# Rows of four experts gathered in one product, and an expert loop of period four on TensorE

## The chip, the cores and the metric

The kernel runs on one core of one Trainium2 chip. The metric is the device time of one execution in microseconds (us). A core has a matrix engine (TensorE; in the profile PE for its products and PEld for its weight loads), VectorE (DVE), ScalarE (ACT), GpSimd (POOL), and SyncE (SP), which here only issues transfers. Sixteen DMA engines move data between HBM and the on-chip memory (SBUF). TensorE writes to eight banks of a second memory (PSUM), 128 partitions by 512 floats each. The engines run their own instruction streams and wait for each other by semaphores.

## The reference

Two layers of a backbone block: three token mixers (which the change leaves alone), then a mixture of experts. The model width is 1024. Layer 0 works on 512 tokens (256 latent, 256 context), layer 1 on 256. Each token goes to two of 32 experts; an expert is a gated product of width 512. Cut to the expert part:

```python
weights = p_grp * top_p                       # two weights for each token
experts = g_top * EXP_PER_GROUP + top_i       # two of 32 experts
xs = h_pad[token_of_slot].reshape(n_blk, MOE_BLK, D)     # rows in the order of the experts
def run_block(args):
    xb, e = args
    return (silu(xb @ w_gate[e]) * (xb @ w_up[e])) @ w_down[e]
ys = lax.map(run_block, (xs, block_expert)).reshape(n_slots, D)
out = zeros((T, D)).at[order // TOP_K].add(ys[dest] * w_sorted[:, None])
```

An expert's weights are 1024 x 1024 (gate and up side by side) and 512 x 1024 floats, 6.3 MB; 32 experts in two layers make 403 MB.

## The kernel before

After the mixers and the router, the normalized token rows stand in SBUF twice, as a rounded part `hr_hi` and a rest `hr_lo` (128 tokens to a tile, `nt` = 4 tiles in layer 0 and 2 in layer 1). `place1` holds for each token and expert the token's place among that expert's rows. Experts are worked on in order, and the first 64 rows (`BLK`) of each are the normal case. Weights stand in two slots: expert e uses slot e % 2, in pieces of 1 MB (four of `wgu` and two of `wd`).

Around each pair of experts:

- VectorE makes `pick` (L1571), a one-hot matrix for each token tile of 2 x 64 columns: column j is the token at place j of the expert.
- TensorE `pick_x` (L761): `pick` stands in the array and row halves of 512 columns move, so that 128 rows (64 of each expert) come to banks 0 and 7, slots on partitions. VectorE copies them to `xs` (L1582, L1583).
- TensorE `turn_x` (L770) turns them into model width on partitions, eight turns of 128 x 128, and VectorE copies the two banks to `xg` (L1586, L1587).

For each expert TensorE does `gate_up` (L777: 64 instructions, 32 weight loads and 32 products), half of the next pair's pick or turn, `turn_h` (L789, 4 instructions) of the hidden rows that ScalarE (L1202) and VectorE (L1645) made, the other half, and `down` (L794, 32 instructions). For the next pair the even expert (s = 0) picks (32 instructions in layer 0) and the odd one (s = 1) turns (16). The two are the body of TensorE's loop (L889), 16 times a layer. ScalarE copies the result (L1206) and sends it to `y_rows` in HBM (L1154).

If an expert has more than 64 rows (L859), `more_slots` (L807) works on 32 further rows at a time before `gate_up`, with waits between its steps: 242 array instructions in layer 0. The body is written out once for rows 65 to 96, and again in a loop for those beyond, which is skipped if there are none (L868). In the profiled execution this path ran four times (L1185, count 4): for experts 17 and 20 of layer 0 and 2 and 7 of layer 1, once each.

SyncE's loop (L460) asks for the weights two experts ahead. Before each piece it waits until TensorE has used that piece of the slot (`gu_used`, L452, and `down_used`, L457). The weights of experts 0 and 1 are asked for at the end of the mixers (L446).

Ahead of a loop stand, on TensorE, `pick_x` and `turn_x` for the first pair (L848 to L852) and, on VectorE, the remaining routing steps (L1597 to L1610). Behind it GpSimd fetches the rows of `y_rows` (L1767).

Of the kernel before, what the change touches and what calls it, by code (L numbers as in the profile page):

```python
# [27 lines left out]
P = 128  # L28
# [27 lines left out]
AHEAD = 4  # L56
PAIRS = NE // 2
LATENT, CONTEXT = slice(0, SEQ), slice(SEQ, NTOK)
# [78 lines left out]
def hybrid_block(nc, t, out, counts=None):  # L137
# [4 lines left out]
    with ctx:  # L142
# [49 lines left out]
        def part(base, kib, size, *dims, dt=F32):  # L192
# [21 lines left out]
        xg, xs = part(ht_flat, 8, 4, KC, P), part(ht_flat, 12, 4)  # L214
# [3 lines left out]
        pick = placed("pick", [P, 4, 2 * BLK], ARENA_AT + 38 * 1024, F32R)  # L218
        ysb, ysb_o = part(arena, 40, 2), part(arena, 42, 1)
# [48 lines left out]
            hr_hi_set hr_lo_set r_exp r_onehot r_pos r_exp_done routed pick_set picko_set dest_set xs_done xs_copied xt_done xt_copied  # L268
# [203 lines left out]
        def _(pe):  # L472
# [115 lines left out]
            for l in range(DEPTH):  # L588
# [172 lines left out]
                def pick_x(half):  # L761

                    for tile in range(nt):
                        for rows in (hr_hi, hr_lo):
                            mm = pe.matmul(ps[:, 7 * half, :], pick[:, tile, :], rows[:, tile, 512 * half:512 * half + 512],  # L765
                                           start=(tile == 0 and rows is hr_hi), stop=(tile == nt - 1 and rows is hr_lo))
                    if half:
                        mm.then_inc(g["xs_done"].sem, 1)

                def turn_x(half):  # L770
                    for c in range(4):
                        at = (4 * half + c) * P
                        mm = pe.transpose(ps[:, 7 * half, c * P:(c + 1) * P], xs[:, at:at + P], ident[:, :])
                    if half:
                        mm.then_inc(g["xt_done"].sem, 1)

                def gate_up(s, slot, landed):  # L777
# [29 lines left out]
                def more_slots(more, slot, landed, s, two):  # L807
# [27 lines left out]
                    for k in range(4):  # L835
                        if k % 2 == 0:
                            pe.wait_ge(wd_in[s][k // 2].sem, (PAIRS * l + two + 1) * 16)
                        for j in range(4):
                            mm = pe.matmul(ps[quarters[j], 6, 0:256], hid_t_o[:, quarters[k]], wd[s][k // 2][:, k % 2, 256 * j:256 * j + 256],
# [6 lines left out]
                pair0, pick0 = (PAIRS + 1) * l, (PAIRS + 2) * l  # L846
# [7 lines left out]
                def expert(e, two, s):  # L854
                    done, landed, slot = NE * l + e, PAIRS * l + two + 1, s
                    n = pe.value_load(n_of[0:1, bass.ds(e, 1)], min_val=0, max_val=NTOK)
                    pe.wait_ge(g["xt_copied"].sem, pair0 + two + 1)
                    pe.nop(nofuse=True)
                    with pe.If(n > BLK):  # L859
                        if s:  # L860
                            pe.wait_ge(g["xs_copied"].sem, pair0 + two + 2)

                        def more_block(b):
                            more_slots(pe.snap(n_more, min_val=0, max_val=64), slot, landed, s, two)
                            pe.reg_add(n_more, n_more, 1)

                        more_block(BLK // MORE)
                        with pe.If(n > BLK + MORE):  # L868
                            with pe.Fori(BLK // MORE + 1, w_all // MORE) as b:
                                with pe.If(n > b * MORE):  # L870
                                    more_block(b)
                                pe.nop(nofuse=True)
# [991 lines left out]
```

## Time and profile before

| | us |
|---|---|
| median of 3 runs | 2012.0 |
| the three | 2002.98, 2012.0, 2014.25 |
| span of the profiled execution | 2003.0 |

| engine | busy us | share |
|---|---|---|
| TensorE products | 1775.8 | 89% |
| TensorE weight loads | 1006.8 | 50% |
| VectorE | 693.7 | 35% |
| ScalarE | 521.1 | 26% |
| GpSimd | 155.9 | 8% |

The page cuts the span into 40 slices of 50 us. The tenths of the DMA engines' busy share and the rate show where transfers fill the time:

```profile
DMA  8346555322345999999999443334388999999993
GB/s 317 132 169 230 190 206 207 110 73 90 100 165 223 421 421 421 421 420 415 408 421 420 146 132 98 100 106 146 121 354 310 421 421 420 421 421 421 420 420 135
```

Slices 13 to 21 are layer 0's expert loop, 30 to 38 that of layer 1. Of the costliest groups these belong to it (line, engine, operation, output<-input, count | busy us, mean ns | idle time before and its cause):

```profile
L784 PE MATMUL ps<-moe,ht 128*64 128x512 f32 x2048 | 473.2, 604 | 57.9 <-DMA moe<-in_w_exp_gate_up_dram 43.5
...
L800 PE MATMUL ps<-moe,arena 128*64 128x512 f32 x1024 | 233.8, 598 | 2.5
...
L765 PE MATMUL ps<-hr_hi,pick 128*128 128x512 f32 x204 | 88.9, 436 | 9.7 <-DVE pick L1571 9.7
L765 PE MATMUL ps<-hr_lo,pick 128*128 128x512 f32 x204 | 82.4, 404 | 0.0
```

Products overlap each other, so the distance between two starts says more than the duration of one. "issue" is time in which an engine waited for nothing that the profile shows.

### The profile page before, as it was taken

The numbers are of one execution on the slowest core, as the hardware profiler recorded it, in microseconds if no ns is written. First come the engines' busy times: TensorE is split into PE (matmuls) and PEld (weight loads), VectorE is DVE, ScalarE is ACT, GpSimd is POOL, SyncE is SP. The second block draws the span as 40 slices with busy tenths as digits, with TensorE's granted clock in tenths as the row PEclk, the third lists the DMA queues.
The fourth block names the chain that finished last, engine by engine and source line by source line (L and its number), as shares of the span: only waits on it lengthen the run. The fifth ranks groups of instructions, "written<-read, shape, count | busy, mean of one in ns | idle before, by whom it ended". The sixth has DMA issues, their size and how long they took to land.

```text
span 2003.0 us, 26586 instructions
## 1 busy us (share of the span) xinstructions
PE 1775.8 (89%) x9291; PEld 1006.8 (50%) x9292; DVE 693.7 (35%) x1455; ACT 521.1 (26%) x1061; POOL 155.9 (8%) x190
## 2 busy tenths in 40 slices
PE   6999899989986999989999599999969999888884
PEld 3766566668753443334343487778823333222322
DVE  3465355444533111111111665673441111111113
ACT  4344444442321111001111454452311111011011
POOL 0063031000000000000000224320000000000000
PEclk9999999999988999999999799999979999999997
DMA  8346555322345999999999443334388999999993
GB/s 317 132 169 230 190 206 207 110 73 90 100 165 223 421 421 421 421 420 415 408 421 420 146 132 98 100 106 146 121 354 310 421 421 420 421 421 421 420 420 135
DMA packets 96048, 550.55 MB, mean 275 GB/s; under 512 B 14162, under 2 KB 15650, under 8 KB 42724
## 3 DMA queue, kind: packets, MB, share of 16 engines
q1 hardware_dynamic: 83108, 526.89, 66.6%
q0 software_dynamic: 4224, 11.35, 2.0%
q10 hardware_dynamic: 8640, 11.28, 1.6%
q8 instruction: 50, 0.82, 0.2%
q14 instruction: 26, 0.21, 0.0%
HBM read 537.15 MB, written 12.32 MB: 274 GB/s over the span
## 4 chain that ended last, share of the span: by engine, by line
PE 65%; DMA 14%; DVE 8%; SPq 5%; ACT 4%; issue 3%; POOL 0%; ACTq 0%; POOLq 0%; DVEq 0%
PE ps L784 14%; DMA moe<-in_w_exp_gate_up_dram 12%; PE ps L493 8%; PE ps L800 8%; PE ps L495 8%; PE ps L494 8%; PE ps L765 4%; SPq L412 3%; PE ps L715 2%; PE ps L642 2%; PE ps L671 2%; PE ps L653 2%; SPq L417 1%; DMA moe<-in_w_mod_dram 1%; DVE w_lo L1302 1%
## 5 line engine op out<-in xcount | busy, mean ns | idle before, releaser
L784 PE MATMUL ps<-moe,ht 128*64 128x512 f32 x2048 | 473.2, 604 | 57.9 <-DMA moe<-in_w_exp_gate_up_dram 43.5
L784 PEld LDWEIGHTS ps<-moe,ht 128*64 128x64 f32 x2048 | 140.9, 138 | 379.6 <-issue 258.7
L1645 DVE TENSOR_TENSOR arena<-aux,ps 128x256 f32<-128x256 f32 x64 | 26.9, 421 | 673.2 <-ACT aux L1202 673.2
L493 PE MATMUL ps<-ht_hi,w_hi 128*128 128x512 f32 (+1 forms) x704 | 252.3, 358 | 2.0 <-ACT arena L1089 1.6
L495 PE MATMUL ps<-ht_hi,w_lo 128*128 128x512 f32 (+1 forms) x704 | 243.7, 346 | 0.0
L494 PE MATMUL ps<-ht_lo,w_hi 128*128 128x512 f32 (+1 forms) x704 | 243.5, 346 | 0.0
L800 PE MATMUL ps<-moe,arena 128*64 128x512 f32 x1024 | 233.8, 598 | 2.5
L1302 DVE TENSOR_TENSOR w_lo<-ws,w_hi 128x1024 fp32r<-128x1024 f32 (+1 forms) x122 | 149.5, 1230 | 222.4 <-ACT w_hi L994 222.3
L994 ACT ACTIVATE w_hi<-ws 128x1024 fp32r<-128x1024 f32 (+1 forms) x122 | 125.2, 1026 | 180.1 <-PE ps L495 146.1
L493 PEld LDWEIGHTS ps<-ht_hi,w_hi 128*128 128x128 f32 x704 | 133.2, 189 | 24.4 <-issue 8.6
L495 PEld LDWEIGHTS ps<-ht_hi,w_lo 128*128 128x128 f32 x704 | 133.1, 189 | 16.9
L494 PEld LDWEIGHTS ps<-ht_lo,w_hi 128*128 128x128 f32 x704 | 133.4, 189 | 15.3
L1206 ACT ACTIVATE arena<-ps 128x512 f32<-128x512 f32 x64 | 38.2, 597 | 370.5 <-PE ps L800 370.5
L800 PEld LDWEIGHTS ps<-moe,arena 128*64 128x64 f32 x1024 | 67.8, 136 | 131.3 <-issue 111.4
L1767 POOL DMA_INDIRECT arena<-y_rows,dest x8 | 8.0, 1001 | 1447.1 <-ACTq L1221 1445.3
L1202 ACT ACTIVATE aux<-ps 128x256 f32<-128x256 f32 x64 | 24.6, 385 | 335.4 <-PE ps L784 335.4
L765 PE MATMUL ps<-hr_hi,pick 128*128 128x512 f32 x204 | 88.9, 436 | 9.7 <-DVE pick L1571 9.7
L765 PE MATMUL ps<-hr_lo,pick 128*128 128x512 f32 x204 | 82.4, 404 | 0.0
L1202 ACT ACT_TABLE_LOAD x32 | 41.1, 1283 | 134.4 <-issue 134.4
L765 PEld LDWEIGHTS ps<-hr_hi,pick 128*128 128x128 f32 x204 | 39.6, 194 | 42.3 <-issue 30.7
L1750 POOL DMA_DIRECT2D aux<-in_rpb_a_dram x64 | 39.8, 634 | 181.2 <-DVE stat L1420 127.5
L653 PEld LDWEIGHTS ps<-ident,moe 128*128 128x128 f32 x320 | 35.0, 143 | 34.4 <-issue 32.6
(252 smaller groups left out, 2159.1 us busy)
## 6 DMA issues: line engine op xcount, KB each, us to landing
moe<-in_w_exp_gate_up_dram SPq DMA_DIRECT2D x256, 1024.0 KB, 20.7
moe<-in_w_exp_down_dram SPq DMA_DIRECT2D x128, 1024.0 KB, 21.4
ws<-in_w_in_dram SPq DMA_DIRECT2D x92, 512.0 KB, 4.2
moe<-in_w_mod_dram SPq DMA_DIRECT2D x29, 1536.0 KB, 6.5
y_rows<-arena ACTq DMA_DIRECT2D x164, 64.0 KB, 5.6
ws<-in_w_branch_dram SPq DMA_DIRECT2D x16, 512.0 KB, 3.5
ws<-in_w_out_dram SPq DMA_DIRECT2D x16, 512.0 KB, 3.6
arena<-in_w_mod_dram SPq DMA_DIRECT2D x3, 1536.0 KB, 19.3
```

Of the source, the lines that this page charges most:

```text
L412: sp.dma_start(wgu[slot][i], e_src(t["w_exp_gate_up"])[:, 2 * i:2 * i + 2]).then_inc(gu_in[slot][i].sem, 16)
L493: pe.matmul(ps[:, bank, 0:cols], w[:, k, :], a_hi, start=(i == 0), stop=False)
L494: pe.matmul(ps[:, bank, 0:cols], w[:, k, :], a_lo, start=False, stop=False)
L495: mm = pe.matmul(ps[:, bank, 0:cols], w_lo[:, slot, k, :], a_hi, start=False, stop=(k == rows[-1]))
L642: mm = pe.matmul(score_bank[:, hh, 0:n], q_of(kind)[HD * hh:HD * hh + HD, pair, q0:q0 + P], kt_of(kind, 2 * pair + hh)[:, keys], start=Tru ...
L653: mm = pe.transpose(prob_bank[:, tile, hh * P:(hh + 1) * P], prob[h % 2][:, hh, tile * P:(tile + 1) * P], ident[:, :])
L765: mm = pe.matmul(ps[:, 7 * half, :], pick[:, tile, :], rows[:, tile, 512 * half:512 * half + 512], start=(tile == 0 and rows is hr_hi), st ...
L784: mm = pe.matmul(ps[BLK * j:BLK * j + BLK, 2, :].rearrange("p (g n) -> p g n", g=2), xg[:, k, BLK * s:BLK * s + BLK], w[k // 2][:, k % 2, ...
L800: mm = pe.matmul(ps[BLK * j:BLK * j + BLK, bank, :], src[:, k % 2, BLK * (k // 2):BLK * (k // 2) + BLK], w[k // 2][:, k % 2, 512 * j:512 * ...
L994: nc.scalar.activation(high_part(i)[:, 0:m], ws[:, slot, 0:m, :], ACT.Copy) \
L1202: nc.scalar.activation(act_g, ps[:, 2, 0:256], ACT.Silu).then_inc(g["silu_done"].sem, 1)
L1302: v.tensor_tensor(w_lo[:, ws_slots[item], 0:m], ws[:, ws_slots[item], 0:m, :], high_part(i)[:, 0:m].bitcast(F32), ALU.subtract).then_inc(g ...
```

## The change

`pick` becomes 4 x 64 columns (`set_four`), and a product now has 128 columns of the rows standing in the array and the 256 one-hot columns moving. The output is already turned: model width on partitions, the slots of four experts in the columns. `turn_x`, `xs` and the copies to it are gone. The eight chunks of the model width are gathered two for each expert (`gather(2 * s)`, `gather(2 * s + 1)`). VectorE holds six of them in `xg_next` and at the fourth expert copies them to `xg` and the last two from PSUM. `gate_up` of the first of four waits for `xg` piece by piece. TensorE's and VectorE's loops have period four; ScalarE's and SyncE's stay at two. On TensorE the large-expert path is now written once, in one loop over all steps of 32 rows from 64 on (14 steps in layer 0, 6 in layer 1), each with its own test. On VectorE and ScalarE it stays as it was.

```diff
-AHEAD = 4
+FOUR = 4
+AHEAD = 2 * FOUR
...
-                def pick_x(half):
+                def gather(chunk):
+
+                    bank, at = 7 * (chunk // 2 % 2), FOUR * BLK * (chunk % 2)
                     for tile in range(nt):
                         for rows in (hr_hi, hr_lo):
-                            mm = pe.matmul(ps[:, 7 * half, :], pick[:, tile, :], rows[:, tile, 512 * half:512 * half + 512],
+                            mm = pe.matmul(ps[:, bank, at:at + FOUR * BLK], rows[:, tile, chunk * P:(chunk + 1) * P], pick[:, tile, :],
...
+                            if s == 0:
+                                pe.wait_ge(g["xg_set"].sem, turned + k // 2 + 1)
...
-                pick_x(0)
-                pick_x(1)
-                pe.wait_ge(g["xs_copied"].sem, pair0 + 1)
-                turn_x(0)
-                turn_x(1)
...
+                for chunk in range(KC):
+                    if chunk in (4, 6):
+                        pe.wait_ge(g["xg_set"].sem, gathered + chunk // 2 - 1)
+                    gather(chunk)
...
-                    pe.wait_ge(g["xt_copied"].sem, pair0 + two + 1)
                     pe.nop(nofuse=True)
                     with pe.If(n > BLK):
                         if s:
...
+                            pe.wait_ge(g["xg_held"].sem, QUADS * FOUR * l + 4 * four + s)
+                        else:
+                            pe.wait_ge(g["xg_set"].sem, gathered + 4 * four + 4)
+                        pe.nop(nofuse=True)
+                        with pe.Fori(BLK // MORE, w_all // MORE) as b:
+                            with pe.If(n > b * MORE):
+                                more_slots(pe.snap(n_more, min_val=0, max_val=64), slot, landed)
+                                pe.reg_add(n_more, n_more, 1)
+                            pe.nop(nofuse=True)
                         pe.nop(nofuse=True)
                     pe.nop()
-                    gate_up(s, slot, landed)
+                    gate_up(s, slot, landed, gathered + 4 * four)
                     if s == 0:
-                        pe.wait_ge(g["pick_set"].sem, pick0 + two + 2)
+                        pe.wait_ge(g["pick_set"].sem, pick0 + four + 2)
                     else:
-                        pe.wait_ge(g["xs_copied"].sem, pair0 + two + 2)
-                    next_pair = turn_x if s else pick_x
-                    next_pair(0)
+                        pe.wait_ge(g["xg_held"].sem, QUADS * FOUR * l + 4 * four + s)
+                    gather(2 * s)
                     pe.wait_ge(g["hid_done"].sem, done + 1)
                     turn_h(hid)
-                    next_pair(1)
+                    gather(2 * s + 1)
...
-                with pe.Fori(0, PAIRS) as two:
-                    for s in range(2):
-                        expert(2 * two + s, two, s)
+                with pe.Fori(0, QUADS) as four:
+                    for s in range(FOUR):
+                        expert(FOUR * four + s, four, s)
...
-                set_pair(0)
-                dve.wait_ge(g["xs_done"].sem, pair0 + 1)
-                copy_xs()
-                set_pair(2)
-                dve.wait_ge(g["xt_done"].sem, pair0 + 1)
-                copy_xg()
+                def gathered_rows(p):
+                    return ps[:, 7 * (p % 2), :].rearrange("p (k n) -> p k n", n=FOUR * BLK)
+
+                done0 = 4 * (QUADS + 1) * l
+                set_four(0)
+                for p in range(4):
+                    dve.wait_ge(g["xg_done"].sem, done0 + p + 1)
+                    v.tensor_copy(xg[:, 2 * p:2 * p + 2, :], gathered_rows(p)).then_inc(g["xg_set"].sem, 1)
+                set_four(FOUR)
...
-                    if s == 0:
-                        dve.wait_ge(g["xs_done"].sem, pair0 + two + 2)
-                        copy_xs()
-                    else:
-                        dve.wait_ge(g["xt_done"].sem, pair0 + two + 2)
-                        copy_xg()
-                        set_pair(e + 3)
...
+                    if s < 3:
+                        dve.wait_ge(g["xg_done"].sem, done0 + 4 * four + s + 5)
+                        v.tensor_copy(xg_next[:, 2 * s:2 * s + 2, :], gathered_rows(s)).then_inc(g["xg_held"].sem, 1)
+                        return
+                    dve.wait_ge(g["xg_held"].sem, QUADS * FOUR * l + 4 * four + 3)
+                    for p in range(3):
+                        v.tensor_copy(xg[:, 2 * p:2 * p + 2, :], xg_next[:, 2 * p:2 * p + 2, :]).then_inc(g["xg_set"].sem, 1)
+                    dve.wait_ge(g["xg_done"].sem, done0 + 4 * four + 8)
+                    v.tensor_copy(xg[:, 6:8, :], gathered_rows(3)).then_inc(g["xg_set"].sem, 1)
+                    dve.sem_inc(g["xg_held"].sem, 1)
+                    set_four(e + FOUR + 1)
```

## Rows read from the trace of the kernel before

**Rows 1.** Stages: length; busy PE, PEld, DVE, ACT, POOL (x count); clock; DMA share; GB/s

```profile
614.00:617.00 3.00, 3.00 (x8) 2.32 (x8) 0.00 (x0) 0.00 (x0) 0.00 (x0) 0.50 0.00 0
...
641.00:650.00 9.00, 7.77 (x38) 2.48 (x36) 0.61 (x2) 0.60 (x1) 0.00 (x0) 1.00 0.87 310
...
653.00:767.00 114.00, 112.08 (x526) 45.90 (x528) 21.83 (x41) 13.59 (x21) 0.00 (x0) 1.00 1.01 421
...
941.00:961.00 20.00, 20.00 (x92) 8.19 (x92) 2.13 (x4) 2.65 (x4) 0.00 (x0) 1.00 1.00 373
...
1521.00:1533.00 12.00, 10.89 (x113) 4.61 (x107) 0.58 (x2) 2.23 (x4) 0.00 (x0) 0.94 0.32 103
...
1560.00:1958.00 398.00, 355.14 (x1675) 124.03 (x1675) 64.35 (x127) 43.87 (x69) 0.00 (x0) 1.00 1.01 421
```

**Rows 2.** The chain that ended last, in order of time: start, length, what

```profile
613.12 6.12 PE ps L765 x16
...
672.31 6.89 PE ps L784 x32
...
684.72 6.87 PE ps L784 x32
...
886.41 7.04 PE ps L784 x32
...
1070.62 26.32 DMA moe<-in_w_exp_gate_up_dram
...
1528.06 7.02 PE ps L784 x32
```

**Rows 3.** SyncE's queue, DMA issues: start, length of the issues, what

```profile
630.58 6.11 SPq L412 DMA_DIRECT2D moe<-in_w_exp_gate_up_dram  x4
...
942.93 5.48 SPq L412 DMA_DIRECT2D moe<-in_w_exp_gate_up_dram  x4
...
1530.12 5.46 SPq L412 DMA_DIRECT2D moe<-in_w_exp_gate_up_dram  x4
```

**Rows 4.** Queue 1 in 612-888, 612-943, 1480-1605 us: packets, MB, share of engines

```profile
q1 hardware_dynamic: 14159, 103.16, 90.4%
q1 hardware_dynamic: 17209, 125.39, 91.5%
q1 hardware_dynamic: 5810, 42.34, 84.8%
```

**Rows 5.** TensorE's products in order of time

```profile
680.12 0.44 PE L791 MATMUL ps<-ident,arena 128*128 128x128 f32 x2 [0.35 <-DVE arena L1645]
...
1445.60 0.28 PE L493 MATMUL ps<-mt_hi,w_hi 128*128 128x256 f32 x1
...
1445.72 0.28 PE L494 MATMUL ps<-mt_lo,w_hi 128*128 128x256 f32 x1
```

**Rows 6.** The one-hot tile's line: ns min/median/max of its two forms, 256 and 512 columns

```profile
L1571 DVE TENSOR_TENSOR pick<-arena,slots x36: 414/553/692, 612.4 to 1962.9; 128x512 fp32r<-128x512 f32 x18, 128x256 fp32r<-128x256 f32 x18
```

**Rows 7.** TensorE's sequencer, branch over the large path: before experts 0, 0, 1; ns, start

```profile
L859 PEldq COMPARE_BRANCH  x1: 3389/3389/3389, 623.2 to 623.2; - x1
L859 PEldq COMPARE_BRANCH  x1: 2796/2796/2796, 1478.3 to 1478.3; - x1
L859 PEldq COMPARE_BRANCH  x1: 6275/6275/6275, 1493.2 to 1493.2; - x1
```

**Rows 8.** TensorE's sequencer, back edge at 654 us, and the inner branch: ns, start

```profile
L889 PEldq ALU_OP  x1: 32/32/32, 654.1 to 654.1; - x1
L889 PEldq COMPARE_BRANCH  x1: 228/228/228, 654.2 to 654.2; - x1
L889 PEldq FUSED_REGOPS  x1: 63/63/63, 654.6 to 654.6; - x1
L868 PEldq COMPARE_BRANCH  x4: 208/210/213, 885.0 to 1601.6; - x4
```

**Rows 9.** Instruction queue from 612 to 660 us: packets, MB, share of engines

```profile
q8 instruction: 5, 0.08, 0.7%
```

More of the change, by code:

```diff
@@ L217, in hybrid_block @@
         pick_o = placed("pick_o", [P, 4, MORE], ARENA_AT + 37 * 1024, F32R)
-        pick = placed("pick", [P, 4, 2 * BLK], ARENA_AT + 38 * 1024, F32R)
-        ysb, ysb_o = part(arena, 40, 2), part(arena, 42, 1)
+        pick = placed("pick", [P, 4, FOUR * BLK], ARENA_AT + 38 * 1024, F32R)
+        ysb, ysb_o = part(arena, 42, 2), part(arena, 45, 1)
         xs_o, xg_o = aux[0:MORE, 2:4, :].rearrange("p a b -> p (a b)"), part(arena, 44, 1)
@@ L759, in _, with gate_up @@
                 pe.wait_ge(g["hr_lo_set"].sem, g["hr_lo_set"].at(l, 2 * nt - 1))
-                def pick_x(half):
+                def gather(chunk):
+                    bank, at = 7 * (chunk // 2 % 2), FOUR * BLK * (chunk % 2)
                     for tile in range(nt):
                         for rows in (hr_hi, hr_lo):
-                            mm = pe.matmul(ps[:, 7 * half, :], pick[:, tile, :], rows[:, tile, 512 * half:512 * half + 512],
+                            mm = pe.matmul(ps[:, bank, at:at + FOUR * BLK], rows[:, tile, chunk * P:(chunk + 1) * P], pick[:, tile, :],
                                            start=(tile == 0 and rows is hr_hi), stop=(tile == nt - 1 and rows is hr_lo))
[L767 to L777, printed above, removed]
+                    if chunk % 2:
+                        mm.then_inc(g["xg_done"].sem, 1)
+                def gate_up(s, slot, landed, turned):
                     w = wgu[slot]
@@ L805, in _, with more_slots @@
                 quarters = [slice(MORE * j, MORE * j + MORE) for j in range(4)]
-                def more_slots(more, slot, landed, s, two):
+                def more_slots(more, slot, landed):
                     pe.wait_ge(g["picko_set"].sem, more + 1)
@@ L883, in expert @@
                     turn_h(hid)
[L884 removed]
+                    gather(2 * s + 1)
                     pe.wait_ge(g["hidt_copied"].sem, done + 1)
                     pe.wait_ge(g["y_copied"].sem, done + 1)
[L887 to L891 removed]
+                    down(4, hid_t, slot, landed)
+                with pe.Fori(0, QUADS) as four:
+                    for s in range(FOUR):
+                        expert(FOUR * four + s, four, s)
@@ L1616, in _, with expert @@
                     dve.reg_mov(n_more, 0)
-                def expert(e, two, s):
+                def expert(e, four, s):
                     done = NE * l + e
@@ L1647, in expert @@
                     v.tensor_copy(hid_t, ps[:, 1, 0:256].rearrange("p (c n) -> p c n", n=P)).then_inc(g["hidt_copied"].sem, 1)
-                    if s == 0:
-                        dve.wait_ge(g["xs_done"].sem, pair0 + two + 2)
-                        copy_xs()
-                    else:
-                        dve.wait_ge(g["xt_done"].sem, pair0 + two + 2)
-                        copy_xg()
-                        set_pair(e + 3)
-                with dve.Fori(0, PAIRS) as two:
-                    for s in range(2):
-                        expert(2 * two + s, two, s)
+                    if s < 3:
[9 more added lines that the diff above has]
+                    set_four(e + FOUR + 1)
+                with dve.Fori(0, QUADS) as four:
+                    for s in range(FOUR):
+                        expert(FOUR * four + s, four, s)
                 def add_tile(tile):
```

42 lines of the change are left out of this document (13 added, 29 removed).

## The prediction

> **What bounds the kernel now.** I read the 40 slices of the page first, then the busy time by stage, then the chain that ended last, then the instructions of each queue. The change touches only the two expert loops (about 613 to 1105 us and 1470 to 1966 us). In them the DMA engines are full: their share is 1.01 at 421 GB/s from 653 us to the end of layer 0's loop and from 1560 to 1958 us [rows 1]. An expert brings six pieces of 1.05 MB, so at 421 GB/s (its output rows travel in the same stream) it takes 14.9 us. TensorE needs 12.4 us for an odd expert (672.31 to 684.72) and some 2 us more for an even one, and the chain near a loop's end is a transfer of gate/up weights that TensorE waits for (at 1070.62) [rows 2]. So inside the loop a TensorE microsecond is worth nothing in itself. It counts only where the transfers run dry, since a piece is asked for only when TensorE has used its slot. The rows to see are three places. At the start of a loop nothing moves until the first slot is released (630.58, [rows 3]). Around the third expert of layer 1, which has more than 64 rows, the DMA share is 0.32 for 12 us [rows 1], and the next release is at 1530.12 [rows 3]. Around expert 20 of layer 0 (941 to 961 us) the rate dips to 373 GB/s [rows 1].
>
> How much was still in flight at such a place: before the release at 888.47, 17 experts had been asked for since 612 us, 107.0 MB, of which 103.2 had moved by 888 [rows 4]: 3.8 MB or 9 us in hand. At 942.93 it was 20 experts, 125.8 MB against 125.4: 1 us in hand, and the 20 us that follow lose 20*(421-373)/421 = 2.3 us. At the second large expert of layer 1 (number 7), 44.0 MB against 42.3: 4 us in hand.
>
> **The change, part by part.** All against the profiled execution (span 2003.0 us, itself the fastest of the three times; the median is 9 us above it, so a shift in the trace is applied to 2012).
>
> *Gather in place of pick and turn.* For four experts of layer 0, TensorE now issues 2*16 products of 512 columns and 2*8 turns; after it, 64 products of 256 columns. A 256-column product of this type follows its predecessor by 0.12 us at full clock [rows 5], so a chunk of eight costs 0.96 us (0.48 in layer 1), two chunks an expert. The first chunk runs while ScalarE and VectorE make the hidden rows, a time in which today's four turns leave the array idle for 0.35 us (at 680.12, [rows 5]). From the odd expert's 12.4 us an expert then comes to about 12.7 us in layer 0 and 12.5 in layer 1. That saves 3 us for every four experts, which the full DMA hides: 0. VectorE's three extra copies and its one-hot tile of 1024 columns end within the 3.6 us of the down product, except before an odd large expert; 0.4 us there.
>
> *Start of a loop, layer 0.* The first one-hot tile grows from 512 to 1024 columns. By the two forms of its line (0.41 and 0.69 us, [rows 6]) that is 1.2 us, so +0.5. [...] After, 64 products start at 613.6: 18 at the low clock (0.24 us) and 46 at 0.12, together 9.9, to 623.5, and the copies run beside them. Now the jump over the code of the large-expert path follows. Its branch started at 623.2, behind the wait for the copies, and took 3.39 us [rows 7], which is why the experts began at 626.6. In steady state the sequencer is 1 to 3 us ahead of the array (the loop-count branch at 885.0 runs 1.4 us before the product at 886.41, [rows 2, 8]), and the new order has no wait ahead of the jump. I take 3 us of it as hidden: first product at 624.1, at the high clock, first release 2.0 us later instead of 3.9: 626.1 against 630.58, -4.4. Nothing hidden and a low clock would give +1. From 641 to 650 us the transfers lost 2.4 us (310 GB/s, [rows 1]) because the second expert also waited for code; I give back 1.6. Layer 0's start: -6.
>
> *The empty iterations.* The body for rows beyond 64 was written twice and the loop around the second was skipped. Now there is one body in a loop of 14 steps (6 in layer 1), of which only one works: 13 (or 5) empty steps on TensorE's queue for each large expert. No row shows one. A step is one taken branch over the body (208 ns), a nop, a register operation (32 ns) and the branch back (208) [rows 8]: 0.5 us by durations. By starts, the loop's own back edge (operation at 654.1, next instruction at 654.6, [rows 8]) takes 0.5 alone, which makes a step 0.9. I take 0.7, the middle. The last products cover 1.4 us. So a large expert costs TensorE 13*0.7-1.4 = 7.7 us more in layer 0 and 5*0.7-1.4 = 2.1 in layer 1. With 0.5 it is 5.1 and 1.1, with 0.9 it is 10.3 and 3.1. Nothing below zero: instructions are only added.
>
> [...]
>
> Layer 0: expert 17 has 9 us in hand and loses 7.7: about nothing. Expert 20 comes later by 7.7, less 1.4 for three quicker experts, plus 0.4 and its own 7.7: its release moves from 942.93 to 957.3. Transfers restart some 1.7 us later at 959.0. Before, they went on as if from 944.0+2.3 = 946.3: +12.7. Layer 0 in all: -6+12.7+0.2 (the last expert's second chunk is 0.3 us longer) = +6.9.
>
> *Layer 1.* The gather is 32 products: 18 at 0.24 and 14 at 0.12, 6.0 us from 1470.0 to 1476.0. The branch took 2.80 us from 1478.3 [rows 7]. In the new order its predecessors are held by the copy of the second pair, to about 1475.7, so it ends at 1478.5, against 1481.1. Expert 0 then runs at the high clock: 12.5. The jump to expert 1 took 6.28 us [rows 7] over two bodies; over one I take 4, of which 3 lie under the down product: +1.1, against 3.6. Experts 0 and 1 end at 1504.6 instead of 1515.1. The large path takes 12.5 + 0.3 + 2.1: expert 2's product at 1519.5 instead of 1528.06 [rows 2]: -8.6. As the transfers had run dry there, all of it counts. With the jumps fully exposed and the low clock it would be +0.5, with both hidden -12. Expert 7 has 4 us in hand and is later by 2.1 + 1.4 (first jump to the fourth copy of the code) - 1: it loses about 1.5. Layer 1: -7.
>
> Sum: +6.9-7.1 = -0.2; nothing else moves. Forecast 2011 us, the profile near 2002.
>
> **The rivals.**
> First, *empty steps are hidden* and cost under 0.4 us. Then no large expert matters: layer 0 gives -6 and the 2.3 us dip back, -8; layer 1 -9: 17 us faster, 1995. For it: the sequencer is seen ahead of the array. Against it: the branch rows.
>
> Second, slower: *a step costs 1.1 us*, as branch and nop each refill the queue. A large expert is 12.9 us in layer 0. Its release at expert 20 moves by 2*12.9-1.0 = 24.8 and the restart by 23.1; expert 17's 9 us are gone too. Layer 0 +17, layer 1 (4.1 per large expert) -3: 14 us slower, 2026. It decides from about 1.0 us a step, just above the 0.9 of the rows.
>
> Third, *the start gains nothing*: the code jumps stay exposed behind the gather. Layer 0 then is +13 and layer 1 near -3, if the warm clock stays: +9, 2021.
>
> Fourth, *the longer loop no longer stays in TensorE's instruction memory*. Now five 16 KB instruction packets come in 612 to 660 us [rows 9] and none from 660 to 1060 us, so the two-expert loop stays. It has some 1,220 array instructions; four experts with one body each have about 1,500. If each expert's jump cost 3.6 us again, it would take 16.3 instead of 14.9 us, 1.4*64 = 90 us slower, 2100. [...]
>
> **How the numbers follow.** Forecast (2011, own range 2002 to 2020): 0.52. Hidden steps 0.16, dear steps 0.17, no gain at the start 0.10, code not resident 0.05. A measurement of this kernel can tell about 0.5%, 10 us, from no change. Faster: the first rival and 0.03 of the forecast's edge, 0.19. Slower: the second and fourth and a little of the third and of the edge, 0.26. Same: 0.55. The range reaches from 1995 to the second rival: 1994 to 2027. It leaves out the fourth rival and the ends of the others.
>
> **What would show it.** In the profile after: 256-column products 0.12 us apart; the first release in layer 0 near 626 and in layer 1 an expert-2 product near 1519; a DMA share of 1.01 for the rest; a hole of some 8 to 12 us before expert 20's release in layer 0 and gaps of several us between the last product of the large path and the gate/up product behind it, 13 branch records each; no instruction packets in the middle of a loop. The forecast is wrong if those gaps are under 3 or over 11 us, if the first expert still starts 3 us behind the last gather, or if instruction packets recur.

## The result and the profile after

| | before | after |
|---|---|---|
| median of 9 runs each, us | 2011.4 (2003.0 to 2014.3) | 2016.7 (2015.4 to 2020.4) |
| span of the profiled execution | 2003.0 | 2014.6 |

The ratio is 1.0035, interval 1.0024 to 1.0046: the change costs 0.35%, 5 to 9 us. I had forecast 2011 and no change. The time lies within the range and within 0.5% of before, but it is measurably slower, and two large terms lie behind the small sum. Layer 0's loop lost twice what I had allowed; layer 1's gained what I had said. The experiments below remove the loss, and the kernel is then 0.8 to 1% faster than before.

The page of the kernel after (tenths and rate in 40 slices of 50.4 us; the instruction queue; the gate/up products):

```profile
DMA  8346555323246999997999533334488999999993
GB/s 315 131 168 229 194 201 213 105 68 100 89 186 255 419 420 421 421 398 318 372 420 421 224 111 100 95 110 131 136 352 318 421 410 421 421 421 421 420 421 137
...
q8 instruction: 52, 0.85, 0.2%
...
L782 PE MATMUL ps<-moe,ht 128*64 128x512 f32 x2048 | 476.8, 603 | 85.2 <-DMA moe<-in_w_exp_gate_up_dram 59.1
```

Three slices in layer 0 leave the full rate: 398, 318 and 372 GB/s stand from 857 to 1008 us, with the large experts 17 and 20 in them. Nothing else of note has moved. The chain of waits in order of time (start, length, what) tells why:

```profile
614.55 9.79 PE ps L768 x64
...
883.17 9.07 issue
892.24 8.56 PE ps L782 x32
...
932.27 3.84 PE ps L811 x16
...
945.60 1.93 PE ps L837 x32
947.53 8.87 issue
956.40 8.90 PE ps L782 x32
...
1488.11 6.04 PE ps L768 x32
...
1507.17 2.41 issue
1509.58 8.81 PE ps L782 x32
...
1535.62 2.79 issue
1538.41 7.11 PE ps L782 x32
```

Behind each large path (L837 is its last line) TensorE stands still for 9 us in layer 0 and 2.8 in layer 1. (The 2.41 us at 1507.17 are something else: the jump to expert 1, whose branch is shown at the end.) Before, the product behind it followed at once: 886.41 there [rows 2] answers to 892.24 here, and 940.88 to 956.40. From the same chain before, the product behind expert 20's large path, which started at 925.95:

```profile
940.88 7.02 PE ps L784 x32
```

TensorE's sequencer in the first gap (operation, count, ns min/median/max, first and last start):

```profile
L862 PEldq COMPARE_BRANCH  x14: 86/218/222, 882.4 to 892.1; - x14
...
L862 PEldq FUSED_REGOPS  x13: 35/35/35, 882.6 to 891.6; - x13
...
L863 PEldq COMPARE_BRANCH  x13: 214/214/214, 882.7 to 891.7; - x13
```

Thirteen branches over the body (L863) and the loop's own tests (L862): the empty steps. From the first to the last are 12 steps in 9.0 us, 0.75 us each. Thirteen make 9.75, and 9.07 of it shows, so the products in flight cover 0.7 us. Then SyncE's queue, the first issue after the releases of the first expert and of 17 and 20 of layer 0, the first and the last of which answer to [rows 3]:

```profile
626.37 5.47 SPq L414 DMA_DIRECT2D moe<-in_w_exp_gate_up_dram  x4
...
895.85 5.46 SPq L414 DMA_DIRECT2D moe<-in_w_exp_gate_up_dram  x4
...
960.26 5.55 SPq L414 DMA_DIRECT2D moe<-in_w_exp_gate_up_dram  x4
```

And the stretches around the gaps (length; busy PE, PEld, DVE, ACT, POOL; granted clock; DMA share; GB/s):

```profile
883.00:892.00 9.00, 0.17 (x4) 0.00 (x0) 0.00 (x0) 0.38 (x1) 0.00 (x0) 0.80 1.01 420
892.00:896.00 4.00, 3.76 (x12) 1.26 (x14) 0.00 (x0) 0.00 (x0) 0.00 (x0) 0.59 0.69 287
...
956.00:960.00 4.00, 3.60 (x10) 1.17 (x12) 0.00 (x0) 0.00 (x0) 0.00 (x0) 0.50 0.00 0
```

Two things are to be seen. Expert 17's gap is bridged by transfers in flight (share 1.01 up to 892), with nothing left over: the rate falls as the gap ends, and around expert 20, where nothing is in hand, the transfers stand (share 0.00) until the release at 960.26. And the products behind the gap run at a granted clock of 0.59 and 0.50, after TensorE had stood idle: microsecond by microsecond it is 1.00 up to 888 us, 0.50 from 889 to 895 and 1.00 again from 896; in the second gap it is 1.00 up to 949 and 0.50 from 950 to 960. That is why the gate/up products took 8.56 and 8.90 us where they took 7.04 and 7.02 before, and it was in none of my terms.

### The profile page after: what moved, and what is told of

Read it like the earlier page. It is cut to its first block, busy times and chain, and to the rows that moved or that the text cites. A ratio compares the mean times of both kernels' runs of the same rounds, so it can differ in the third digit from the quotient of the medians.

```text
span 2014.6 us, 26958 instructions
## 1 busy us (share of the span) xinstructions
PE 1764.4 (88%) x9475; PEld 1017.7 (51%) x9476; DVE 671.9 (33%) x1423; ACT 521.1 (26%) x1061; POOL 155.1 (8%) x190
## 4 chain that ended last, share of the span: by engine, by line
PE 60%; DMA 17%; SPq 7%; DVE 7%; issue 4%; ACT 4%; POOL 0%; ACTq 0%; POOLq 0%; DVEq 0%
DMA moe<-in_w_exp_gate_up_dram 15%; PE ps L782 11%; PE ps L495 8%; PE ps L497 8%; PE ps L496 8%; PE ps L798 7%; SPq L414 4%; PE ps L768 3%; SPq L419 2%; PE ps L717 2%; PE ps L644 2%; PE ps L673 2%; PE ps L655 2%; DMA moe<-in_w_mod_dram 1%; PE ps L553 1%
## 5 line engine op out<-in xcount | busy, mean ns | idle before, releaser
L798 PE MATMUL ps<-moe,arena 128*64 128x512 f32 x1024 | 235.5, 602 | 1.3
L496 PEld LDWEIGHTS ps<-ht_lo,w_hi 128*128 128x128 f32 x704 | 134.5, 191 | 15.3
L768 PE MATMUL ps<-pick,hr_hi 128*128 128x256 f32 x432 | 124.2, 316 | 10.5 <-DVE pick L1564 10.5
L798 PEld LDWEIGHTS ps<-moe,arena 128*64 128x64 f32 x1024 | 68.2, 137 | 123.1 <-issue 105.8
L768 PEld LDWEIGHTS ps<-pick,hr_hi 128*128 128x128 f32 x432 | 84.4, 195 | 62.6 <-issue 57.0
L768 PE MATMUL ps<-pick,hr_lo 128*128 128x256 f32 x432 | 111.5, 287 | 0.0
L768 PEld LDWEIGHTS ps<-pick,hr_lo 128*128 128x128 f32 x432 | 84.8, 196 | 0.0
```

What stands on the lines that cost most here:

```text
L496: pe.matmul(ps[:, bank, 0:cols], w[:, k, :], a_lo, start=False, stop=False)
L768: mm = pe.matmul(ps[:, bank, at:at + FOUR * BLK], rows[:, tile, chunk * P:(chunk + 1) * P], pick[:, tile, :], start=(tile == 0 and rows is ...
L798: mm = pe.matmul(ps[BLK * j:BLK * j + BLK, bank, :], src[:, k % 2, BLK * (k // 2):BLK * (k // 2) + BLK], w[k // 2][:, k % 2, 512 * j:512 * ...
```

## How the spans divide

I cut each profile at the start of the first one-hot product of a layer and at the start of the layer's last down product. For the kernel before these are 613.12, 1100.82, 1469.75 and 1961.71 us.

| kernel | span | layer 0's loop | between | layer 1's loop |
|---|---|---|---|---|
| before | 2003.0 | 487.7 | 368.9 | 492.0 |
| before again (e8) | 2006.0 | 488.5 | 370.8 | 492.3 |
| after | 2014.6 | 503.0 | 370.6 | 485.0 |
| e1 after, loop bounded by n | 1991.2 | 482.5 | 370.2 | 480.5 |
| e11 the same again | 1992.0 | 482.5 | 370.7 | 480.4 |
| e5 before, loop bounded by n | 1991.2 | 483.3 | 369.2 | 484.7 |
| e12 the same again | 1998.8 | 484.4 | 375.2 | 483.8 |
| e2 before with empty steps | 2017.0 | 504.4 | 369.3 | 488.7 |
| e4 after, twice the empty steps | 2048.8 | 522.1 | 374.4 | 498.7 |
| e9 after, short products in the gap | 2020.9 | 503.3 | 373.0 | 489.4 |
| e10 e1 and 0.95 us more an expert | 1995.2 | 485.4 | 370.3 | 483.2 |

## The experiments

My theory after the result: the gather does what it should, and the empty steps of the rewritten large-expert loop cost more than it gives. The rivals: the gather itself (64 and 32 small products, more copies) is dear; the longer code is; or TensorE's extra time in the full-rate stretches counts after all.

### The empty steps taken away (e1, e11)

```diff
-                        with pe.Fori(BLK // MORE, w_all // MORE) as b:
-                            with pe.If(n > b * MORE):
-                                more_slots(pe.snap(n_more, min_val=0, max_val=64), slot, landed)
-                                pe.reg_add(n_more, n_more, 1)
+                        with pe.Fori(BLK, n, MORE):
+                            more_slots(pe.snap(n_more, min_val=0, max_val=64), slot, landed)
+                            pe.reg_add(n_more, n_more, 1)
```

The loop now ends at the expert's own number of rows, read from the register, and needs no test inside. The rest of the change stays.

> The changed kernel, but the loop of the large path ends at the expert's own row count (start 64, end n, step 32) and has no test inside: no empty steps, one body. Theory (the empty steps, 13 or 5 of 0.75 us each, and the low clock behind them are what the change lost): the gap of some 9 us behind the large path is gone in layer 0 and that of 2.7 us in layer 1; layer 0's last transfer lands about 5 us earlier than in the kernel before, layer 1 gains about 11 us; span near 1987 against 2003.0 before and 2014.6 after, ratio to before about 0.992. Rival (the gather of narrow products or the loop of period four costs the time): the span stays above 2003.

Measured: 1991.4 us, ratio 0.990 (0.9883 to 0.9918). The chain of e1 has no gap behind the large paths of layer 0:

```profile
881.72 2.02 PE ps L837 x32
883.74 7.02 PE ps L782 x32
...
937.48 7.02 PE ps L782 x32
```

and SyncE's queue and the stretch from 941 to 961 us, against 373 GB/s before [rows 1] (the same columns as above):

```profile
885.80 5.47 SPq L414 DMA_DIRECT2D moe<-in_w_exp_gate_up_dram  x4
...
939.53 5.48 SPq L414 DMA_DIRECT2D moe<-in_w_exp_gate_up_dram  x4
...
941.00:961.00 20.00, 20.00 (x110) 9.26 (x108) 3.08 (x6) 1.93 (x4) 0.00 (x0) 1.00 1.02 420
```

The products stand at full clock, and both releases come sooner than before (888.47 in its timeline, and 942.93 [rows 3]). Layer 0's loop falls by 20.5 us against the kernel after, layer 1's by 4.5. So the empty steps, with what follows them, cost about 25 us in these profiles, and the gather costs nothing that could explain the loss. My expected span, 1987, was 4 us too low. I ran the same kernel again beside e12, below.

> The gather of four with the loop bounded by n, timed beside the pairs with the loop bounded by n. In the two traces layer 0 was equally long and layer 1 some 4 us shorter with the gather. Theory: the gather is worth 4 us, 0.2%. Rival (it is worth nothing that can be measured): within 1 us of the next kernel.

Measured: 1994.0, ratio 0.9919 (0.9901 to 0.9936), the same loops within 0.1 us.

### The empty steps alone (e2)

The kernel before, with its pairs and its picks and turns, but the large path written once, in the loop with the test:

```diff
...
-                        more_block(BLK // MORE)
-                        with pe.If(n > BLK + MORE):
-                            with pe.Fori(BLK // MORE + 1, w_all // MORE) as b:
-                                with pe.If(n > b * MORE):
-                                    more_block(b)
-                                pe.nop(nofuse=True)
+                        pe.nop(nofuse=True)
+                        with pe.Fori(BLK // MORE, w_all // MORE) as b:
+                            with pe.If(n > b * MORE):
+                                more_slots(pe.snap(n_more, min_val=0, max_val=64), slot, landed, s, two)
+                                pe.reg_add(n_more, n_more, 1)
+                            pe.nop(nofuse=True)
```

> The kernel before, with nothing changed but TensorE's large path: one body in a loop of 14 (layer 1: 6) steps with a test in each, as in the changed kernel. Theory: each large expert of layer 0 has a gap of about 9 us behind its last product, expert 20 of layer 0 is released some 20 us later, layer 1 loses about 3; span near 2026, ratio about 1.011. Rival (the steps alone are harmless, it is their place in the loop of four): within 5 us of 2003.

Measured: 2020.1, ratio 1.0053 (1.0033 to 1.0074). Its chain:

```profile
882.36 8.61 issue
947.25 8.71 issue
```

The same gaps, without the gather (and 2.72 us in layer 1). Layer 0's loop grew by 16.7 us, as the kernel after's did by 15.3: this part of the change alone accounts for layer 0. I had expected a span of 2026, and it is 2017.0. What I had left out is that layer 1's loop fell by 3.3 us: with one body in place of two, its first two branches over the body took 3.36 and 0.34 us, where before they took 2.80 and 6.28 [rows 7].

### Twice the empty steps (e4)

```diff
-                        with pe.Fori(BLK // MORE, w_all // MORE) as b:
+                        with pe.Fori(BLK // MORE, 2 * w_all // MORE - 3) as b:
```

> The changed kernel with twice the empty steps: 26 in layer 0 and 10 in layer 1 for each large expert. Theory with 0.75 us a step: gaps of about 19 and 6.4 us, release of expert 20 in layer 0 another 19.5 us later, layer 1 another 5; span near 2039. If the low clock behind the gap were the larger part of the loss, doubling would add little beyond 10 us.

Measured: 2050.4, ratio 1.0195 (1.0176 to 1.0213). The gaps in the chain of e4 (that of expert 20 is 18.59), with two of the products behind them:

```profile
880.50 18.83 issue
...
1556.00 6.51 issue
1562.51 9.89 PE ps L782 x32
...
1641.69 6.36 issue
1648.05 9.79 PE ps L782 x32
```

18.83-9.07 = 9.76 us for 13 more steps and 6.51-2.79 = 3.72 for 5: 0.75 and 0.74 us a step, which settles the price. Layer 0's loop grew by 19.1, as expected: once nothing is in hand, each microsecond of a gap counts in full, 2*9.76 = 19.5. The span is 2048.8 where I had expected 2039: the miss lies in layer 1, +13.7 where I had 5, and between the loops, +3.8. Two gaps of 3.7 make 7.4 of the 13.7. The low clock makes 6.1 more: the products behind the longer gaps took 9.89, 7.71 and 9.79 us, where after the same three took 7.11, 7.05 and 7.10. So most of the miss is the term that I had left out again; why the time between the loops grew stays open.

### The clock behind the gap (e6, e9)

To see what the low clock costs, TensorE must be kept busy in the gap. First with one 512-column product of plain fp32 type in each step, whose result nobody reads:

```diff
                         with pe.Fori(BLK // MORE, w_all // MORE) as b:
+                            pe.matmul(ps[:, 5, :], ident[:, :], slots1[:, 0:512], start=True, stop=True)
                             with pe.If(n > b * MORE):
```

> The changed kernel with one product of 512 columns into an unused bank in each of the 14 (6) steps: the gap behind the large path stays as long, but TensorE works in it. Theory (the low clock behind the gap is a term of its own): the gate/up product behind the gap takes 6.9 instead of 8.6 us, the release comes 2.0 instead of 3.6 us after its start, layer 0 ends some 3 us earlier, span near 2011. Rival (the clock costs nothing, or the extra products lengthen the gap): 2014 or more.

Measured: 2025.3, ratio 1.0079 (1.0057 to 1.0100). The clock held, 1.00 from 948 to 964 us, but the product takes 0.86 us (two parts 0.43 apart), longer than the step of 0.75 that it should fill, and the gap grew to 11.3 us. So I tried two shorter ones (the type of the gather's operands, 0.23 us each at their pace in the kernel):

```diff
+                            for _ in range(2):
+                                pe.matmul(ps[:, 5, :], hr_hi[:, 0, 0:P], hr_hi[:, 0, 0:512], start=True, stop=True)
```

> The changed kernel with two short products (0.23 us each) in each step of the large path's loop, so that TensorE works in the gap and a step still takes 0.75 us. Theory (the low clock behind the gap costs 3.5 us in layer 0 beside the empty steps): gap of 9 to 10 us, clock 1.00 in it, release 2.1 us behind the first gate/up product instead of 3.6 and 3.9, layer 0 some 5 us shorter than in the changed kernel (1.5 and 1.6 in the products behind, 1.8 in the last release), span near 2010. Rival (the clock is no term): 2014 to 2015.

Measured: 2021.4, ratio 1.0054 (1.0034 to 1.0074). The branch records and SyncE's issue behind the gap:

```profile
L865 PEldq COMPARE_BRANCH  x13: 214/214/214, 883.6 to 894.0; - x13
...
896.66 5.47 SPq L414 DMA_DIRECT2D moe<-in_w_exp_gate_up_dram  x4
```

Twelve steps now take 10.4 us, 0.87 each, as they did in e6 (883.8 to 894.2): a product or two in a step lengthen it by 0.12, the short ones too. With the clock at 1.00 (884 to 894 us) the gate/up products behind the gaps take 7.0 and 7.1 us and the release comes 2.1 us behind their start, where after it was 895.85-892.24 = 3.6. What the clock gives (1.5 us at each) the longer steps take: layer 0's loop is 503.3 against 503.0. So the clock's price is shown in its pieces, not in the total; both totals missed my expectation (spans 2022.7 and 2020.9, where I had 2011 and 2010).

### Is TensorE's time in the loop free? (e7, e10)

e1 with needless products at the end of each expert, first two of plain fp32 type:

```diff
                     down(4, hid_t, slot, landed)
+                    for _ in range(2):
+                        pe.matmul(ps[:, 5, :], ident[:, :], slots1[:, 0:512], start=True, stop=True)
```

> The kernel with the loop bounded by n, plus two needless products of 512 columns behind each expert's down product, some 0.86 us for each of 64 experts, 55 us of TensorE in all. Theory (inside the loops the transfers are the bound, TensorE counts only up to the last place where they run dry): layer 0 some 3 us later (17 to 20 experts, within the backlog, only the three behind expert 17 count), layer 1 some 2 us (expert 0 to 2), span near 1995 against 1991.2. Rival (TensorE's time per expert is what the loops follow): 2035 to 2046.

Measured: 2029.3, ratio 1.0100 (1.0079 to 1.0121), and a span 33 us above e1's. The two took 1.9 us an expert, not the 0.9 that I had meant to add, 122 us in all. An expert came to 14.8 us on TensorE, level with the transfers' 14.9, so that nothing was left to make up a delay. With seven turns of 128 columns instead:

```diff
+                    for _ in range(7):
+                        pe.transpose(ps[:, 5, 0:P], ident[:, :], ident[:, :])
```

> The kernel with the loop bounded by n, plus seven needless turns of 128 columns behind each down product, some 0.95 us for each expert, 61 us in all (in the earlier one it was 1.9 us each, 123 us, which took all of TensorE's room). An expert then takes 13.7 us against 14.9 of its transfers. Theory: only the three experts behind number 17 of layer 0 and the first two of layer 1 count, at most the release of 20 is 3 us later and that of expert 2 in layer 1 2 us: span 1994 to 1998. Rival (TensorE's time counts in full, or by half): 2020 or more.

Measured: 1999.1, ratio 0.9948 (0.9928 to 0.9968), span +4.0 over e1, median +5.1 over e11, which was timed beside it. The added work of one expert, and the full-rate stretch from 712 to 850 us:

```profile
708.88 0.99 PE L881 MATMUL ps<-ident 128*128 128x128 f32 x7
...
712.00:850.00 138.00, 134.68 (x707) 59.59 (x705) 20.78 (x42) 15.63 (x24) 0.00 (x0) 1.00 1.02 421
```

TensorE is busy for 134.7 of 138 us and the transfers lose nothing: 64 times 0.95 = 61 us of TensorE's time cost 4 to 5. Nearly free, then, up to the transfers' own pace. It also says what the gather's saving on TensorE (0.7 us an expert) can be worth inside the loop: next to nothing.

### Code length (e3)

The kernel after with its large path written as before, once for rows 65 to 96 and once in a loop that is skipped, in each of the four experts (some 2,460 array instructions in the loop, against 1,500):

```diff
...
+                        more_block(BLK // MORE)
+                        with pe.If(n > BLK + MORE):
+                            with pe.Fori(BLK // MORE + 1, w_all // MORE) as b:
+                                with pe.If(n > b * MORE):
+                                    more_block(b)
+                                pe.nop(nofuse=True)
```

> The changed kernel with the large path written as before: one body outside, one in a guarded loop, so no empty steps, but some 2,460 array instructions in layer 0's loop of four instead of 1,500. If the code stays in the instruction memory: like the loop bounded by n, span 1987 to 1991. [...]

Measured: 2334.4, ratio 1.160 (1.1572 to 1.1629). The page's instruction queue, the branch over the large path from 654 to 1083 us, and a gap from the chain of e3:

```profile
q8 instruction: 221, 3.62, 0.6%
...
L856 PEldq COMPARE_BRANCH  x21: 80/6181/7157, 654.2 to 1082.3; - x21
...
694.70 11.10 issue
```

Four times the instruction packets (52 after), and branches of 6.2 us in the median where they stay at 0.2. The two-body form, at two experts a turn, is what the kernel before has; at four a turn, by these packets and branches, it no longer stays in TensorE's instruction memory. My direction was right and my size, an estimate of 40 to 90 us more and a span of 2030 to 2080, was far too small. This is my fourth rival, made true: the one-body loop of the kernel after does stay (52 packets on the whole page). The rewriting of the loop was thus needed to go to four experts; only its form was wrong. The runs show 1,500 array instructions that stay and 2,460 that don't; where between them the limit lies they don't show.

### The loop's new form without the gather (e5, e12)

The kernel before, its pairs, picks and turns kept, one body bounded by n:

```diff
-                        def more_block(b):
+                        pe.nop(nofuse=True)
+                        with pe.Fori(BLK, n, MORE):
                             more_slots(pe.snap(n_more, min_val=0, max_val=64), slot, landed, s, two)
                             pe.reg_add(n_more, n_more, 1)
-
-                        more_block(BLK // MORE)
...
```

> The kernel before (pairs picked and turned, period two), with only the large path written as one body in a loop that ends at the expert's row count. Theory (the shorter code, not the gather, brings most of the gain at the start of the loops: the branch over one body took 0.4 us where it took 3.4 over two): layer 0's experts start some 3 us earlier and the first release comes some 5 us earlier, layer 1 gains about 5; span near 1993, ratio about 0.993. Rival (the one product in place of pick and turn brings it): the span stays at 2000 or more, and only the kernel with the gather of four reaches 1991.

Measured: 1995.1, ratio 0.9931 (0.9914 to 0.9949). Its branch over the large path before the first two experts of layer 0, and before the first three of layer 1:

```profile
L859 PEldq COMPARE_BRANCH  x2: 390/408/427, 621.5 to 635.8; - x2
...
L859 PEldq COMPARE_BRANCH  x3: 77/336/3562, 1472.8 to 1501.1; - x3
```

Where the kernel before pays 3.39 us at layer 0's start, and 2.80 and 6.28 at layer 1's [rows 7], this one pays 0.4, and one branch of 3.6. So most of e1's gain is the shorter code, not the gather. Side by side with e11:

> Pairs picked and turned, period two, with the loop bounded by n, timed on the same chip as the gather of four with the same loop. Theory: some 4 us slower than that one, some 14 faster than the kernel before. Rival: equal to it.

Measured: 1998.9, ratio 0.9937 (0.9919 to 0.9955), against e11's 1994.0. The gather is worth 4.9 us here, 0.2%, and 3.7 by e1 and e5, which were not timed side by side. The intervals overlap, so this is at the edge of what can be told. The table puts it in layer 1 (480.5 and 480.4 against 484.7 and 483.8), and there ahead of expert 2's product, which comes 46.6 and 46.4 us behind the layer's first product against 50.8 and 50.4. In layer 0 the loops differ by 0.8 and 1.9. Between the loops, where the gather has no part, e12 is 4.5 us longer than e11; the spans alone would put the gather at 6.8.

### The kernel before once more (e8)

> The kernel before, unchanged, for a second profile: the one read had a time of 2002.98 us, the lowest of its runs, whose median is 2011. If the extra time of the usual runs lies in the mixers or in the rate of the transfers, every stage is longer by a little; if it lies in one place (the start, the first code of a loop), that place shows it.

Measured: 2008.0, span 2006.0. The time stands 2.0 us above the span; after it is 2016.7 and 2014.6. By that my profile of before, 2003.0, belongs to about 2005, 6 us under the median. The 3 us to e8 are spread over the parts, 1.9 of them between the loops. What makes the kernel before vary over 11 us, where after keeps within 5, stays open.

## Why the prediction was wrong

**The step that failed** is layer 0's term. I had -6 for the start and +12.7 for the empty iterations, +6.9 in all, and layer 0's last down product came 16.7 us later. The cover of the empty steps was mis-sized (1.4 us for a measured 0.7), the low clock of the products behind them was put at nothing (1.5 to 1.9 us each time), and the 1.6 us of the early bubble did not come back.

**What bounds the kernel** was right: full transfers, TensorE counting only where they run dry. e10 shows the first half (61 us of TensorE's time cost 4 to 5), e7 what becomes of it when the margin is gone (122 us cost 33).

**Layer 1: -7.1 forecast, -7.0 measured.** Counted from the layer's first product, expert 2's product stands at 1538.41-18.36 = 1520.05, against 1519.5 forecast. Its pieces balanced rather than fitted. The first jump was hidden altogether (the first gate/up product 2.7 us sooner than I had it); the second was not: 2.41 us show, not 1.1, and the products behind it took 8.81 us at a low clock.

**Layer 0: +6.9 forecast.** The last down product moved by 1117.53-1100.82 = 16.7. The 9.8 between them, step by step in the order of the chain:

| step as forecast | measured | us short |
|---|---|---|
| first gather starts at 613.6 | 614.55; the larger one-hot tile took its 0.5 us, as forecast, the rest lies ahead of the loop | 0.9 |
| start and early bubble give 6 by expert 17 | with the 0.9: 3.3, the large path at 869.65 against 872.95 | 1.8 |
| 17's empty steps 7.7 | 9.07 | 1.4 |
| three experts behind 17 quicker by 1.4 | slower by 0.5 (40.03 against 39.54 from product to large path) | 1.9 |
| 20's large path and steps 8.1 longer | 932.27 to 956.40, 24.13 against 14.93: 9.2 | 1.1 |
| release 2.05 behind the product | 960.26-956.40 = 3.86 | 1.8 |
| 156.4 us from 20's release to the end | 157.3 | 0.9 |

Three causes carry most of it. *The price of a step*: I had taken 0.7 out of 0.5 to 0.9, and it was 0.75 (e4), which is close; but I had 1.4 us of cover from the last products (from the inner branch at 885.0, ahead of the product at 886.41), and only 0.7 was there. At two experts that is the 1.4 and 1.1. *The clock*: I had costed what the gap takes and not what stands behind it. The granted clock fell from 1.00 to 0.50 while TensorE was idle, which made the next 32 products 1.5 and 1.9 us longer, and so each release that waits for the first of them 1.6 and 1.8 later. In the table that is 1.5 of the 1.9 (e1, at full clock, is quicker than before by 1.05 there) and the whole 1.8 at the release. My layer-1 forecast had weighed the low clock at the gather, so the effect was known to me, and I didn't ask where else the change would bring it about. *The early bubble*: I gave back 1.6 us, and nothing came back. The stretch of 20 us from the first release on, before (630.58) and after (626.37):

```profile
630.58:650.58 20.00, 18.77 (x84) 7.61 (x82) 2.13 (x4) 0.98 (x2) 0.00 (x0) 0.98 0.89 329
...
626.37:646.37 20.00, 17.94 (x84) 7.03 (x82) 4.74 (x19) 2.26 (x3) 0.00 (x0) 0.91 0.83 300
...
635.93 5.24 PE ps L798 x16
```

At 329 GB/s the transfers lose 20*(421-329)/421 = 4.4 us, at 300 they lose 5.7. The second expert's wait for code is gone, as I had said, but TensorE now stands still for 2.06 us before the first `turn_h` (634.55), since ScalarE loads its function table (1.28 us) only at 632.36, behind the product, where before it did so at 629.19, beside it. The down product behind that (L798, above) then takes 5.24 us at a granted clock that falls to 0.50 from 636 to 638 us, where it took 3.7, and the down weights' slot is released 13.3 us behind the first release instead of 11.8. This comes with the gather: e1 has the load at 633.17, behind the product, and e5 at 627.53, beside it. Why ScalarE begins so late stays open. In the table that makes 1.6 + 1.4, less the 0.7 by which the first release beat the forecast counted from its own gather: 2.3 for the 1.8; for the 0.5 between them I have no row.

**The steps that held.** The first release: 626.1 forecast, 626.37 measured, and the first gate/up product at 624.25 against 624.1. The jump over the code is hidden, as I had said, but it had also become short, 0.37 us where I had 3.39 with 3 hidden; so this row says little for my reason. The one-hot tile: 1.2 forecast, 1.23 measured. The first gather: I had 9.9 us, with 18 products 0.24 us apart at the low clock. In the profile of before the granted clock is 0.50 up to about 617.5 us, 4.4 us behind the first pick, and those 4.4 us hold 18 such products. After, the products start 0.21 us apart up to 618.77, at 0.50 up to 618 us, and then 0.12 apart, and the 64 take 9.79. No instruction packets recur once the first four experts are through (two in 660 to 880 us, none from there to 1105). The gap in layer 0: under 11 us and over 3, as the forecast's own bounds asked, 13 records; in layer 1, with 5 empty steps, it is 2.79 and 2.67.

**The rivals.** Hidden steps: ruled out by the gaps. Steps of 1.1 us: the price was 0.75, and nothing shows a refill of the queue in it (no instruction packet falls in 880 to 1105 us); yet its forecast of +14 for the profile comes nearest to the +11.6 measured, since clock, cover and bubble did what the dear step was to do. No gain at the start: no, 4.2 us at the first release. Code not resident: no, and e3 shows it at four times my price.

**The total.** Profile against profile the change costs 11.6 us, median against median 5.4, and by the ratio 7.0. I had called the profiled execution the fastest of the three and carried my shift over to the median; a profile 6 us under the median (e8) makes the difference of the whole spans about 6 us too large. The loops are hardly touched by it: they lie within 1 us of e8's, and together they grew by 8.3 us. That the median stands only 5.7 us above my 2011 is partly luck: in the profiles, from which the sum was made, I had -0.2 and it is +11.6.

**What I had not looked for.** That the shorter code was worth more than the gather. I had costed the branch over one body at 4 us, 3 of them hidden, in layer 1, and at 3.39 us, 3 of them hidden, in layer 0, but never asked what one body would give by itself. By e5 and e12 it is worth 0.69 and 0.63%, 13 to 14 us.

## What to carry over

A loop with a fixed bound and a test inside is paid for on the engine's queue for each step that does nothing, here 0.75 us times 13; bound it by the value itself (`Fori(BLK, n, MORE)`), and the same kernel goes from 0.35% slower to 0.8 to 1% faster (e11, e1). When an edit opens a gap on TensorE, cost the gap, then the low clock of the products behind it (here 0.50 to 0.59, 1.5 and 1.9 us for 32 products), then the release that waits for them (1.6 and 1.8 us later), and ask how much the transfers have in hand there. Code that is skipped isn't free either: the first branch of layer 0 took 3.39 us over two bodies and 0.39 over one (e5), and with two bodies in a loop of four the branches took 6.2 in the median and the kernel 16% more than before (e3). What it adds to a loop's length is to be counted before a loop is unrolled further.

## What the runs showed of the hardware

- A step of an empty loop takes 0.75 us (e4), while its instructions' durations add up to 0.214+0.218+0.035+0.036 = 0.50.
- The branch over the large path costs 0.2 us in steady state and 0.37 at layer 0's start in the kernel after, but 5.18 once in layer 1, over code of the same length (TensorE's sequencer, before expert 0 of layer 0 and before expert 1 of layer 1):

```profile
L856 PEldq COMPARE_BRANCH  x1: 370/370/370, 623.2 to 623.2; - x1
...
L856 PEldq COMPARE_BRANCH  x1: 5180/5180/5180, 1504.3 to 1504.3; - x1
```

- The clock's fall doesn't go by the gap's length alone. After 2.41 us idle at 1507.17 the next 32 products took 8.81 us, at a granted clock of 0.81; after 2.79 us at 1535.62 they took 7.11, and after 2.84 us in e1, at 1487.76, 7.10, both at 1.00. In e4 only 1.97 us idle, at 1528.00, stood before another 8.81, at 0.80. What tells them apart stays open.
- Plain fp32 products of 128 rows and 512 columns follow one another by 0.86 us (e6; two of them took 1.91 in e7), nearly four times the 0.23 us between products of the gather's type (e9).
